# The last block of a hybrid encoder kernel: its output projection split into a GLA half and a convolution half

## The chip, the core and the metric

The kernel runs on one core of one Trainium2 chip. The metric is the device time of one execution in microseconds (us), lower being better; three executions of the kernel before took 1037.42, 1040.89 and 1041.53 us.

## What is computed

One step of an encoder layer over 2048 prompt frames and 64 sample frames of width 1024. A normed input goes through one input projection; three groups of heads work on parts of it; each is gated, and one output projection joins them. Cut to the parts that matter here:

```python
def mixer_layer(x, ...):
    proj = rmsnorm(x, norm_g) @ w_in
    ...
    y_attn = band_attention(q, k_all, v_all, sinks, q_pos0) * jax.nn.silu(ag)
    o, s_fin = gla_chunked(gq * GLA_DK ** -0.5, gk, gv, log_a, gla_s0)
    y_gla = rmsnorm(o, gla_g).reshape(B, L, GLA_VDIM) * jax.nn.silu(gg)
    u = cv * jax.nn.sigmoid(cgl)
    c = depthwise_conv(u_all, conv_w) + conv_b            # 31 taps over time, 256 channels
    c = jax.nn.silu(layernorm(c, ln_g, ln_b)) @ w_pw + b_pw
    y_conv = c * jax.nn.silu(cg)
    y = jnp.concatenate([y_attn, y_gla, y_conv], axis=-1) @ w_out
    return x + y, ...
```

The output projection is a sum over the rows of `w_out`: 512 rows belong to attention, 256 to GLA (gated linear attention) and 256 to the convolution.

## The kernel before

It makes two passes. The first works through tiles of 128 frames: norm, attention and the attention rows of the output projection, whose result, with `x` added, is stored in the output. The second works through `NB` = 8 blocks of 256 frames: the projections of GLA and convolution, both mixers, and the other 512 rows of `w_out`, whose result is added to what the first pass stored. Each fp32 product is made of three products of rounded halves (hi by hi, hi by lo, lo by hi), so one bank of the output projection, 128 frames by 512 columns, takes 12 matmuls: four row groups `k` of 128 (0 and 1 are GLA, 2 and 3 convolution), three products each. A block has four such banks (two tiles of frames, two halves of the columns).

Each engine has its own program, written out by hand in a loop over `b` from 0 to `NB`, and runs it strictly in that order; semaphores join them. In round `b` an engine interleaves the work of block `b` ("cur") with the end of block `b - 1` ("done", "prev"). In the last round, `b` = 8, nothing is current: what is left is the end of the last block alone, as a chain through four engines. In the order of that chain, with the functions that issue it:

- `o_sums`, `o_rinv`, `o_norm`: sums, inverse root and scaling of the GLA output (VectorE, GpSimd, VectorE); between them VectorE does the last 14 of the 62 convolution steps of the block (`conv(p, 48, 52)`, `conv(p, 52, 62)`), into `acc`.
- `conv_T`: four TensorE transposes of `acc` into bank `S0`; `o_T`: four of the normed GLA output `on` into `T2`.
- `ln_stats`, `ln_rinv`: layer norm statistics (VectorE, GpSimd).
- `y_gla`, `y_hi`, `y_lo`: the gated GLA output and its two halves `ybg` (tiles `ybgh`, `ybgl`; VectorE, ScalarE, VectorE).
- `ln_scale`: the scaled layer norm, written over `on` (its name there is `cn`) once `ybgl` is done; `cn_T`: four transposes of it into `S1`.
- `conv_silu`, `conv_gate`: scale, tanh and product (ScalarE, VectorE); `pointwise`: the product with `w_pw` into `T2`.
- `y_conv`, `y_hi`, `y_lo`: the gated convolution output and its halves `ybc` (`ybch`, `ybcl`).
- `output_b`: the four banks of the output projection, each with all 12 matmuls; `add`: the sum with the rows loaded into `res`; `store_out_b`: the store, issued by SyncE.

The `J` banks are handed round by a list (`ORDER`), three of them, each filled again once VectorE has emptied it. `o_T` before waits in TensorE's program behind `conv_T`, and every output matmul behind both halves:

```python
                if i == 0 and h == 0:
                    pe.wait_ge(yg_lo, groups_before(b + 1))
                    pe.wait_ge(yc_lo, groups_before(b + 1))
```

Of the kernel before, what the change touches and what calls it, by code (L numbers as in the profile page):

```python
# [33 lines left out]
P = 128  # L34
D = 1024
# [9 lines left out]
CW = 31  # L45
# [16 lines left out]
NB = SEQ // 256  # L62
WIDE = 256 + DEC
U0, U1 = HIST, HIST + 256 + HIST
UB = U1 + DEC
# [122 lines left out]
def build(nc, ins, consts, x_T, outs):  # L188
# [13 lines left out]
    with es:  # L202
# [57 lines left out]
        eb = ExitStack()  # L260
        xbraw = sb("xbraw", [P, KT, WIDE], F32, eb)
        eb.close()
        xbl = sb("xbl", [P, KT, WIDE], F32R)
# [111 lines left out]
        k_taken = sem("gla_k_taken")  # L375
        xb_loaded, params_ready = sem("x_pair_loaded"), sem("params_ready")
        states_stored, u_stored, u_copied = sem("states_stored"), sem("u_stored"), sem("u_copied")
        gv_taken, lr_psum, lr_T = sem("v_taken"), sem("lowrank_psum"), sem("lowrank_T")
# [142 lines left out]
        def load_res_b(b, i):  # L521
# [3 lines left out]
            nc.sync.dma_start(res[n % 2][rows, :], src).then_inc(B.res_loaded[n % 2], 16)  # L525

        def store_out_b(b, i):
            n = tile_no(b, i)
            for h in range(2):
                cols = slice(h * 512, (h + 1) * 512)  # L530
                nc.sync.wait_ge(B.out_added, 2 * n + h + 1)
                rows, dst = out_rows(b, i, cols)
                nc.sync.dma_start(dst, res[n % 2][rows, cols]).then_inc(B.out_stored[n % 2], 16)

# [111 lines left out]
        def go_count(g):  # L646

            gi, _, _, own = g
            return own[-1] + 1 if gi < 2 else tile_no(gi - 1, own[-1]) + 1

        def on_y(g):
# [10 lines left out]
        def bank_of(kind, b, i):  # L662

            return J[BANK[kind, b, i]]

# [9 lines left out]
        def empty_bank(kind, b, i):  # L675

            n = ORDER.index((kind, b, i))
            if n >= 3:
                nc.tensor.wait_ge(*emptied(*ORDER[n - 3]))
            return bank_of(kind, b, i)  # L680
# [12 lines left out]
        def _(sp):  # L693
# [59 lines left out]
            for b in range(NB + 1):  # L753
# [37 lines left out]
        def _(pool):  # L791
# [57 lines left out]
            for b in range(NB + 1):  # L849
                for g in groups(b - 1):  # L850
                    o_rinv(g)
                for g in groups(b - 1):
                    ln_rinv(g)
                if b < NB:
                    for n in range(4):
                        gate(b, n)


        @block.scalar
        def _(act):  # L860
# [223 lines left out]
            def conv_silu(g):  # L1084
                gi, off, w, own = g
                if gi == 0:
                    act.wait_ge(consts_b, N_CONSTS_B)
                bank = T[0] if own == (2,) else S[1]
                act.wait_ge(cnT_psum, gi + 1)
# [20 lines left out]
            for b in range(NB + 1):  # L1110
                cur, done = b < NB, groups(b - 1)
                for g in done:
# [40 lines left out]
                if cur:  # L1153
                    take_kend(b)
                    if b == 0:
                        act.wait_ge(zeros_b, 5)
                    q_blocks(b)
                if b + 1 < NB:
                    split_pair_hi(b + 1, 0)
                    split_pair_hi(b + 1, 1)  # L1160
# [3 lines left out]
        def _(dve):  # L1164
# [238 lines left out]
            def y_gla(g):  # L1403
                gi, off, w, own = g
                b = max(gi - 1, 0)
                dve.wait_ge(oT_psum, gi + 1)
                dve.wait_ge(gate_done, 4 * b + 2)
                nc.vector.scalar_tensor_tensor(on_y(g), T[2][:, :].rearrange("p (j n) -> p j n", n=256)[:, :, 0:w],
                                               glagain[:, 0:1], ggate[:, :, off:off + w], ALU.mult, ALU.mult).then_inc(
                                                   yg_ready, 1)  # L1410
# [19 lines left out]
            def ln_scale(g):  # L1430
# [3 lines left out]
                dve.wait_ge(ln_r, gi + 1)  # L1434
                dve.wait_ge(yg_lo, gi + 1)
                for n, i in enumerate(own):
                    last = nc.vector.tensor_scalar(cn[rows, i, :], bank[rows, 256 * n:256 * n + 256], mv[rows, i, 0:1],
                                                   rs[rows, i:i + 1], ALU.subtract, ALU.mult)
# [96 lines left out]
            def add(b, i, h):  # L1535
                n = SLOT["out", b, 2 * i + h]
                m = tile_no(b, i)
                rows = slice(DEC, P) if i == 2 else slice(0, P)
                if h == 0:
                    dve.wait_ge(B.res_loaded[m % 2], 16 * (m // 2 + 1))  # L1540
                dve.wait_ge(slot_done, n + 1)
                dst = res[m % 2][rows, h * 512:(h + 1) * 512]
                nc.vector.tensor_tensor(dst, bank_of("out", b, 2 * i + h)[rows, :], dst, ALU.add).then_inc(B.out_added, 1)
# [7 lines left out]
            for b in range(NB + 1):  # L1551
                p = b - 1
                cur, prev, done = b < NB, b > 0, groups(b - 1)
                for g in done:
                    o_sums(g)
                if prev:
                    conv(p, 48, 52)
# [4 lines left out]
                if cur and b > 0:  # L1562
                    glu(b, 0)
                if prev:
                    conv(p, 52, 2 * CW)
# [15 lines left out]
                if cur:  # L1581
                    conv(b, 0, 3)
                if b == 0:
# [5 lines left out]
                if cur:  # L1589
                    conv(b, 3, 16)  # L1590
                for g in done:
                    if g[3] != (2,):
                        conv_gate(g)
                if cur:
                    conv(b, 16, 18)
                    logit_parts(b)
# [3 lines left out]
                if cur:  # L1600
                    conv(b, 18, 22)
                    decay_sums(b)
# [6 lines left out]
                if cur:  # L1609
                    conv(b, 22, 30)  # L1610
                if b == 1:
# [3 lines left out]
                if cur:  # L1615
                    k_scaled(b)
                    conv(b, 30, 33)
                    q_scaled(b)
                    conv(b, 33, 36)
                    q_full(b)  # L1620
# [4 lines left out]
                if cur:  # L1625
                    conv(b, 36, 40)
                if b == 0:
# [6 lines left out]
                if b == 0:  # L1634
# [6 lines left out]
                    state(b, 2)  # L1641
                    conv(b, 40, 48)
                elif cur:
                    if b + 1 < NB:
                        split_pair_lo(b + 1, 0)
                    add(p, 1, 0)
                    if b + 1 < NB:
                        split_pair_lo(b + 1, 1)
                    conv(b, 40, 42)
# [14 lines left out]
        def _(pe):  # L1664
# [163 lines left out]
            def output_b(b, i, h):  # L1828
# [12 lines left out]
                last.then_inc(slot_done, 1)  # L1841

            def o_T(g):
                gi, off, w, own = g
                pe.wait_ge(go_n, gi + 1)
                need(pe, yg_ready, gi)
                rows = min(w, P)
                for n, i in enumerate(own):
                    for j in range(CJ):
                        last = nc.tensor.transpose(T[2][:, j * 256 + n * P:j * 256 + n * P + rows],  # L1850
                                                   on[0:rows, i, j * P:(j + 1) * P], ident[0:rows, 0:rows])
                last.then_inc(oT_psum, 1)

            def conv_T(g):
# [4 lines left out]
                if own == (2,):  # L1859
                    pe.wait_ge(yg_ready, gi + 1)  # L1860
                rows = min(w, P)
                for n, i in enumerate(own):
# [6 lines left out]
            def cn_T(g):  # L1869
                gi, off, w, own = g  # L1870
                bank = T[0] if own == (2,) else S[1]
                pe.wait_ge(cn_ready, gi + 1)
                rows = min(w, P)
                for n, i in enumerate(own):
                    for j in range(CJ):
                        last = nc.tensor.transpose(bank[:, j * 256 + n * P:j * 256 + n * P + rows],
                                                   cn[0:rows, i, j * P:(j + 1) * P], ident[0:rows, 0:rows])
                last.then_inc(cnT_psum, 1)

            def pointwise(g):  # L1880
                gi, off, w, own = g
                pe.wait_ge(cs_ready, gi + 1)
                pe.wait_ge(yg_ready, groups_before(max(gi - 1, 0) + 1))
                need(pe, yc_ready, gi)
                pe.wait_ge(cn_ready, groups_before(max(gi - 1, 0) + 1))
                for j in range(CJ):
                    for k in range(CJ):
# [77 lines left out]
            for b in range(NB + 1):  # L1965
                p = b - 1
                cur, prev, done = b < NB, b > 0, groups(b - 1)
                if cur and b > 0:
# [137 lines left out]
```

## Time and profile before

| what | value |
|---|---|
| median of three executions | 1040.89 us (1037.42 to 1041.53) |
| the profiled execution, its own time | 1040.45 us |
| its span in the profile | 1038.7 us |
| TensorE busy | 965.1 us, 93% of the span |
| VectorE busy | 771.2 us, 74% |
| mean granted TensorE clock | 0.964 of full |

The span runs from the first to the last instruction on record; the time of the execution is 1.75 us more than it. [...] In rows of matmuls, busy times of neighbours overlap, so that the start of one to the start of the next is what each costs.

### The profile page before, as it was taken

The page shows a single profiled execution, that of the slowest core. Times are in us where ns is not written, and L with a number is a line of the kernel's source. Part 1 is how long each engine was busy: PE and PEld are TensorE (multiplying, and loading weights), DVE is VectorE, ACT ScalarE, POOL GpSimd, SP SyncE. Part 2 cuts the span into 40 slices and gives each one's busy share as a digit, 9 for nine tenths or more (in the row PEclk, how much of TensorE's full clock was granted, in tenths as well). Part 3 has the DMA queues.
Part 4 walks back from the last instruction along what each step waited for, and adds up shares of the span by engine and source line. Part 5 has one row for each costly group of instructions (what it writes and reads, how often), then busy time and mean ns, then how long its engine had stood idle before and what let it go on. Part 6 is the DMA issues. An engine that isn't in the chain of part 4 may idle for free.

```text
span 1038.7 us, 15969 instructions
## 1 busy us (share of the span) xinstructions
PE 965.1 (93%) x5835; PEld 842.1 (81%) x5835; DVE 771.2 (74%) x1864; ACT 466.2 (45%) x1131; POOL 186.2 (18%) x216
## 2 busy tenths in 40 slices
PE   6769999999999999997989887999999999999956
PEld 5657888888888888886987776998989898989945
DVE  6477777777777777778679677788888888878772
ACT  7266666556656655556654034041423324150400
POOL 0312211222211222210012131020202111121210
PEclk9879999999999999999999798999999999999977
DMA  9412222222222222134342102303030212111021
GB/s 311 172 56 102 102 102 102 94 100 102 102 102 102 102 103 81 62 107 115 95 127 66 47 22 90 93 1 122 1 105 19 71 52 69 54 58 65 1 84 40
DMA packets 57437, 88.37 MB, mean 85 GB/s; under 512 B 9648, under 2 KB 33968, under 8 KB 57360
## 3 DMA queue, kind: packets, MB, share of 16 engines
q1 hardware_dynamic: 57360, 87.36, 25.6%
q8 instruction: 46, 0.75, 0.3%
q14 instruction: 31, 0.25, 0.1%
HBM read 60.80 MB, written 26.60 MB: 84 GB/s over the span
## 4 chain that ended last, share of the span: by engine, by line
PE 79%; DVE 13%; ACT 2%; issue 2%; DMA 2%; POOL 1%; SPq 1%; DVEq 0%; ACTq 0%; POOLq 0%
PE J L619 20%; PE J L1680 18%; PE J L1839 9%; PE J L634 8%; DVE acc L1374 4%; PE J L1824 3%; PE T L1780 3%; PE S L1792 3%; PE S L1748 3%; PE T L1717 2%; PE T L1888 2%; PE S L1960 1%; DMA wraw<-in_w_in 1%; DVE wlo L460 1%; PE T L1726 1%
## 5 line engine op out<-in xcount | busy, mean ns | idle before, releaser
L1374 DVE SCALAR_TENSOR_TENSOR acc<-ub,cwh,acc 128x256 f32<-128x256 f32 (+1 forms) x480 | 222.9, 529 | 0.3
L619 PE MATMUL J<-whi,xhi 128*128 128x512 f32 (+1 forms) x408 | 150.7, 369 | 9.9 <-DVE wlo L460 9.9
L1680 PE MATMUL J<-xbh,whi 128*128 128x256 f32 (+1 forms) x512 | 151.8, 297 | 2.9 <-issue 2.9
L1680 PE MATMUL J<-xbl,whi 128*128 128x256 f32 (+1 forms) x512 | 148.0, 289 | 0.0
L1680 PE MATMUL J<-xbh,wlo 128*128 128x256 f32 (+1 forms) x512 | 147.8, 289 | 0.0
L619 PE MATMUL J<-whi,xlo 128*128 128x512 f32 (+1 forms) x408 | 146.9, 360 | 0.0
L619 PE MATMUL J<-wlo,xhi 128*128 128x512 f32 (+1 forms) x408 | 146.9, 360 | 0.0
L1680 PEld LDWEIGHTS J<-xbh,whi 128*128 128x128 f32 x512 | 98.8, 193 | 6.0 <-issue 5.5
L1680 PEld LDWEIGHTS J<-xbl,whi 128*128 128x128 f32 x512 | 99.0, 193 | 0.2
L1680 PEld LDWEIGHTS J<-xbh,wlo 128*128 128x128 f32 x512 | 98.7, 193 | 0.0
L619 PEld LDWEIGHTS J<-whi,xhi 128*128 128x128 f32 x408 | 78.0, 191 | 20.9 <-DVE xlo L594 9.9
L619 PEld LDWEIGHTS J<-whi,xlo 128*128 128x128 f32 x408 | 77.6, 190 | 12.8
L619 PEld LDWEIGHTS J<-wlo,xhi 128*128 128x128 f32 x408 | 78.1, 192 | 10.3
L925 ACT ACTIVATE sc<-sc,nmx 128x256 f32<-128x256 f32 x136 | 67.6, 500 | 34.5 <-DVE nmx L1202 34.5
L1196 DVE CUSTOM_DVE_ANT_0 sc<-S,bias,sinks 128x256 f32<-128x256 f32 (+1 forms) x136 | 59.2, 471 | 16.6 <-PE S L1748 16.5
L1292 DVE TENSOR_TENSOR ptlo<-T,pthi 128x512 fp32r<-128x512 f32 x68 | 43.9, 687 | 23.5 <-ACT pthi L931 23.5
L584 POOL TENSOR_TENSOR xraw<-xraw,rb 128x1024 f32<-128x1024 f32 x17 | 40.6, 2386 | 103.7 <-ACT rb L578 103.7
L634 PE MATMUL J<-whi,yhi 128*128 128x512 f32 x136 | 56.5, 415 | 0.0
L634 PE MATMUL J<-wlo,yhi 128*128 128x512 f32 x136 | 53.7, 394 | 0.0
L634 PE MATMUL J<-whi,ylo 128*128 128x512 f32 x136 | 53.6, 394 | 0.0
L1780 PE MATMUL T<-ident,sc 128*128 128x128 f32 x272 | 41.9, 289 | 9.6 <-DVE sc L1285 9.6
L1780 PEld LDWEIGHTS T<-ident,sc 128*128 128x128 f32 x272 | 32.8, 145 | 20.0 <-DVE sc L1285 13.5
(235 smaller groups left out, 2226.3 us busy)
## 6 DMA issues: line engine op xcount, KB each, us to landing
out<-res SPq DMA_DIRECT2D x64, 256.0 KB, 2.0
x_normed_scratch<-xraw SPq DMA_DIRECT2D x17, 512.0 KB, 2.9
xraw<-xT SPq DMA_DIRECT2D x16, 512.0 KB, 3.5
xtok<-in_x_prompt SPq DMA_DIRECT2D x16, 512.0 KB, 5.1
res<-in_x_prompt SPq DMA_DIRECT2D x16, 512.0 KB, 5.8
xbraw<-x_normed_scratch SPq DMA_DIRECT2D x16, 512.0 KB, 5.1
res<-out SPq DMA_DIRECT2D x16, 512.0 KB, 4.2
wraw<-in_w_in SPq DMA_DIRECT2D x52, 128.0 KB, 2.5
```

The lines of the kernel that those rows point to most:

```text
L584: nc.gpsimd.tensor_tensor(xraw[t.par][:, :, :], xraw[t.par][:, :, :], rb[:, :].unsqueeze(1).to_broadcast([P, KT, P]), ALU.mult).then_inc(x ...
L619: last = nc.tensor.matmul(bank[:, 0:width], x[x_slot(ps, t)][:, k, :], w, start=(k == 0 and n == 0), stop=(k == KT - 1 and n == 2))
L634: last = nc.tensor.matmul(bank[:, :], y[:, k, :], w, start=(k == 0 and n == 0), stop=(k == 3 and n == 2))
L925: last = nc.scalar.activation(sc[:, h, :], sc[:, h, :], ACT.Exp, bias=nmx[:, h:h + 1], accum_out=esum[:, h:h + 1])
L1196: nc.vector.tensor_tensor_reduce(out=sc[:, h, cols], in0=S[n % 2][:, e * 256:(e + 1) * 256][:, cols], in1=bias[:, h, b0:b0 + 256][:, cols] ...
L1292: nc.vector.tensor_tensor(ptlo[:, k % 2, :], T[k % 3][:, :], f(pthi[:, k % 2, :]), ALU.subtract).then_inc(pt_lo, 1)
L1374: nc.vector.scalar_tensor_tensor(acc[:, j, 0:frames], src, w, acc[:, j, 0:frames], ALU.mult, ALU.add).then_inc(conv_step, 1)
L1680: last = nc.tensor.matmul(bank[:, 0:w], wt, x[:, k, 0:w], start=(k == 0 and m == 0), stop=(k == KT - 1 and m == 2))
L1748: last = nc.tensor.matmul(S[n % 2][:, e * 256:(e + 1) * 256], qT[:, h, :], kT[:, h // GROUP, o, :], start=(o == 0), stop=(o == 1))
L1780: last = nc.tensor.transpose(bank[:, j * P:(j + 1) * P], sc[:, GROUP * g + j, n * P:(n + 1) * P], ident[:, :])
L1792: last = nc.tensor.matmul(S[g][:, :], vcat[n][:, g, :], pt[:, n, :], start=(n == 0 and m == 0), stop=(n == 1 and m == 1))
L1839: last = nc.tensor.matmul(bank[:, :], y[:, k % 2, at:at + P], wt, start=(k == 0 and m == 0), stop=(k == 3 and m == 2))
```

## The change

TensorE's last round is a function of its own, `output_end`. It transposes the GLA output first, then the convolution; it begins the output projection with the GLA rows of three banks as soon as `ybgl` is ready; then come `cn_T`, the GLA rows of the fourth bank, `pointwise`, and at the end the convolution rows of all four banks. So that four sums can be open at once, the fourth takes `S0` in place of a `J` bank. `o_T` goes into `T1`, `cn_T` into `T0`, and the scaled layer norm is written into `acc`. The residual rows of the last block are loaded into the idle input buffer `xbraw` (as `res_end`) in round 7, in place of `res` in round 8. The rest of the chain of the last block moves, on ScalarE, VectorE and GpSimd, from round 8 of the loop to the end of round 7.

```diff
@@ SyncE, round 7
-                for i in tiles(p)[0:2]:
+                for i in tiles(p)[0:2] if b < NB else []:
                     load_res_b(p, i)
...
+                if b == NB - 1:
+                    sp.wait_ge(slot_done, SLOT["gq", b, 0] + 1)
+                    for i in range(2):
+                        load_res_end(i)
@@ VectorE, end of round 7
+                elif b == NB - 1:
+                    g = groups(b)[0]
+                    add(p, 1, 0)
+                    conv(b, 40, 42)
+                    state(b, 0)
+                    conv(b, 42, 45)
+                    add(p, 1, 1)
+                    conv(b, 45, 48)
+                    state(b, 1)
+                    o_sums(g)
+                    conv(b, 48, 52)
+                    o_norm(g)
+                    conv(b, 52, 2 * CW)
+                    ln_stats(g)
+                    y_gla(g)
+                    y_lo(g, on_y(g), ybg, 4.0, yg_hi, yg_lo)
+                    ln_scale(g)
+                    conv_gate(g)
+                    y_conv(g)
+                    y_lo(g, cl[:, :, 0:256], ybc, 0.25, yc_hi, yc_lo)
@@ TensorE
+            def output_end(b):
+
+                o_T(groups(b)[0])
+                conv_T(groups(b)[0])
+                pe.wait_ge(yg_lo, groups_before(b + 1))
+                for s in (0, 1, 2):
+                    output_half(empty_bank("out", b, s), s // 2, s % 2, (0, 1))
+                cn_T(groups(b)[0])
+                output_half(empty_bank("out", b, 3), 1, 1, (0, 1))
+                pointwise(groups(b)[0])
+                pe.wait_ge(yc_lo, groups_before(b + 1))
+                for s in range(4):
+                    output_half(bank_of("out", b, s), s // 2, s % 2, (2, 3)).then_inc(slot_done, 1)
+
+            def output_half(bank, i, h, ks):
+
+                for k in ks:
+                    hi, lo = weights(W_OUT + k * D + h * 512, 512)
+                    yh, yl = (ybg, ybc)[k // 2]
+                    for m, (y, wt) in enumerate(((yh, hi), (yh, lo), (yl, hi))):
+                        last = nc.tensor.matmul(bank[:, :], y[:, k % 2, i * P:(i + 1) * P], wt,
+                                                start=(k == 0 and m == 0), stop=(k == 3 and m == 2),
+                                                skip_group_check=True)
+                return last
```

TensorE's program from the last GLA product of block 7 on, before (`S<-ident,acc` is `conv_T`, `T<-ident,on` is `o_T`, `S<-ident,on` is `cn_T`, `T<-cth,params` is `pointwise`, the `J` rows are `output_b`; the rows behind the last shown repeat its pattern for three more banks):

```order
L1960 MATMUL S<-gvt,asb 128x64 x4
L1865 MATMUL S<-ident,acc 128x128 x4
L1850 MATMUL T<-ident,on 128x128 x4
L1876 MATMUL S<-ident,on 128x128 x4
L1888 MATMUL T<-cth,params 128x256 x4
L1839 MATMUL J<-whi,ybgh 128x512
L1839 MATMUL J<-wlo,ybgh 128x512
L1839 MATMUL J<-whi,ybgl 128x512
...
L1839 MATMUL J<-whi,ybch 128x512
L1839 MATMUL J<-wlo,ybch 128x512
L1839 MATMUL J<-whi,ybcl 128x512
```

The same place now (each "..." stands for more matmuls of the three rows ahead of it, 18 in all in the first case, 6 in the second; `T<-ident,acc` is now `cn_T`, since the scaled norm lies in `acc`):

```order
L2046 MATMUL S<-gvt,asb 128x64 x4
L1930 MATMUL T<-ident,on 128x128 x4
L1947 MATMUL S<-ident,acc 128x128 x4
L1915 MATMUL J<-whi,ybgh 128x512
L1915 MATMUL J<-wlo,ybgh 128x512
L1915 MATMUL J<-whi,ybgl 128x512
...
L1960 MATMUL T<-ident,acc 128x128 x4
L1915 MATMUL S<-whi,ybgh 128x512
L1915 MATMUL S<-wlo,ybgh 128x512
L1915 MATMUL S<-whi,ybgl 128x512
...
L1974 MATMUL T<-cth,params 128x256 x4
L1915 MATMUL J<-whi,ybch 128x512
```

Of the 48 output matmuls 24 now stand ahead of `pointwise`, and 18 of these ahead of `cn_T`.

VectorE's program from the last ten convolution steps on, before:

```order
L1374 SCALAR_TENSOR_TENSOR acc<-ub,cwh,acc 128x256 [waits conv_step] x10
L1423 BN_STATS bst<-S 128x6 [waits cT_psum]
L1427 BN_AGGR mv<-bst 128x2 [waits ln_step]
L1408 SCALAR_TENSOR_TENSOR on<-T,params,ggate 128x512 [waits gate_ready_b,gla_oT_psum]
L1415 SCALAR_TENSOR_TENSOR ybgl<-on,ybgh 128x2x256 [waits gla_y_hi]
L1437 TENSOR_SCALAR on<-S,mv,rs 128x256 [waits gla_y_lo,ln_rinv]
```

And now:

```order
L1404 SCALAR_TENSOR_TENSOR acc<-ub,cwh,acc 128x256 [waits conv_step] x10
L1453 BN_STATS bst<-S 128x6 [waits cT_psum]
L1457 BN_AGGR mv<-bst 128x2 [waits ln_step]
L1438 SCALAR_TENSOR_TENSOR on<-T,params,ggate 128x512 [waits gate_ready_b,gla_oT_psum]
L1445 SCALAR_TENSOR_TENSOR ybgl<-on,ybgh 128x2x256 [waits gla_y_hi]
L1467 TENSOR_SCALAR acc<-S,mv,rs 128x256 [waits gla_y_lo,ln_rinv]
```

Nothing has moved here: VectorE's program has the same instructions in the same order from its first to its last, and only the tiles that `ln_scale` and the last four `add` write are others. The same holds for ScalarE and GpSimd.

## Rows read from the trace of the kernel before

**Rows 1.** The page: the granted clock in 40 equal slices, in tenths of full.

```profile
PEclk9879999999999999999999798999999999999977
```

**Rows 2.** Stretches: length, busy PE, PEld, DVE, ACT, POOL; PEclk, DMA share, GB/s.

```profile
939.40:995.00 55.60, 55.60 (x395) 51.20 (x395) 44.43 (x109) 14.93 (x37) 9.50 (x12) 1.00 0.11 39
995.00:1038.70 43.70, 22.67 (x87) 17.40 (x85) 19.74 (x44) 3.50 (x6) 3.03 (x4) 0.73 0.16 55
```

**Rows 3.** The chain that ended last: start us, length us, what.

```profile
963.85 0.43 PE S L1876 x4
...
970.78 1.73 PE T L1888 x8
...
981.00 2.75 PE J L1839 x12
...
1003.55 3.97 DVE acc L1374 x10
...
1011.10 0.70 DVE ybgl L1415
...
1011.89 1.01 DVE on L1437 x2
...
1012.95 1.13 PE S L1876 x4
...
1016.56 3.80 PE T L1888 x8
...
1020.38 0.89 DVE cl L1453 x2
...
1022.79 12.70 PE J L1839 x48
...
1035.51 0.69 DVE res L1543
```

**Rows 4.** The timeline of the last 35 us: start us, us, engine, line, what.

```profile
1008.47 1.06 PE L1850 MATMUL T<-ident,on 128*128 128x128 f32 x4
...
1009.68 0.72 DVE L1408 SCALAR_TENSOR_TENSOR on<-T,params,ggate 128x512 f32<-128x512 f32 x1
...
1023.35 0.63 PE L1839 MATMUL J<-wlo,ybgh 128*128 128x512 f32 x1
...
1025.49 0.59 PE L1839 MATMUL J<-whi,ybch 128*128 128x512 f32 x1
...
1026.38 0.39 PE L1839 MATMUL J<-whi,ybch 128*128 128x512 f32 x1
...
1035.09 0.39 PE L1839 MATMUL J<-whi,ybcl 128*128 128x512 f32 x1
```

**Rows 5.** Short stretches around changes of the granted clock, columns as in group 2.

```profile
27.00:28.00 1.00, 0.00 (x0) 0.00 (x0) 0.17 (x1) 0.47 (x3) 0.74 (x2) 1.00 0.51 149
...
37.00:38.00 1.00, 0.39 (x4) 0.19 (x2) 0.56 (x1) 1.00 (x5) 0.00 (x0) 1.00 0.00 0
...
39.00:40.00 1.00, 0.00 (x0) 0.00 (x0) 1.00 (x1) 0.00 (x0) 1.00 (x1) 0.73 0.97 385
40.00:41.00 1.00, 0.14 (x1) 0.17 (x2) 0.91 (x2) 0.00 (x0) 0.56 (x1) 0.50 1.07 414
...
46.00:47.00 1.00, 1.00 (x5) 0.78 (x5) 0.00 (x0) 0.27 (x2) 0.57 (x2) 0.86 0.92 324
...
70.16:73.57 3.41, 3.41 (x14) 3.02 (x13) 2.67 (x6) 2.51 (x6) 0.56 (x1) 0.50 0.02 5
...
1002.00:1002.50 0.50, 0.00 (x0) 0.00 (x0) 0.12 (x1) 0.00 (x0) 0.50 (x1) 0.52 0.08 17
...
1025.50:1026.00 0.50, 0.50 (x3) 0.40 (x2) 0.00 (x0) 0.00 (x0) 0.00 (x0) 0.59 0.00 0
```

**Rows 6.** The page: DMA issues of the second pass, KB each, us to landing.

```profile
out<-res SPq DMA_DIRECT2D x64, 256.0 KB, 2.0
...
res<-out SPq DMA_DIRECT2D x16, 512.0 KB, 4.2
```

More of the change, by code:

```diff
@@ L261, in build @@
         xbraw = sb("xbraw", [P, KT, WIDE], F32, eb)
+        res_end = [xbraw[:, :, :].rearrange("p k n -> p (k n)")[:, i * D:(i + 1) * D] for i in range(2)]
         eb.close()
@@ L649, in go_count, with cn_of @@
             return own[-1] + 1 if gi < 2 else tile_no(gi - 1, own[-1]) + 1
+        def cn_of(g, i):
+            return acc[:, i, 0:256] if g[0] == END else cn[:, i, :]
         def on_y(g):
@@ L662, in bank_of @@
         def bank_of(kind, b, i):
-            return J[BANK[kind, b, i]]
+            return S[0] if (kind, b, i) == ("out", NB - 1, 3) else J[BANK[kind, b, i]]
         def emptied(kind, b, j):
@@ L677, in empty_bank @@
             n = ORDER.index((kind, b, i))
-            if n >= 3:
+            if n >= 3 and (kind, b, i) != ("out", NB - 1, 3):
                 nc.tensor.wait_ge(*emptied(*ORDER[n - 3]))
@@ L849, in _ @@
             for b in range(NB + 1):
-                for g in groups(b - 1):
+                for g in groups(b - 1) if b < NB else []:
                     o_rinv(g)
-                for g in groups(b - 1):
+                for g in groups(b - 1) if b < NB else []:
                     ln_rinv(g)
@@ L856, in _ @@
                         gate(b, n)
+                if b == NB - 1:
+                    o_rinv(groups(b)[0])
+                    ln_rinv(groups(b)[0])
         @block.scalar
@@ L1087, in conv_silu @@
                     act.wait_ge(consts_b, N_CONSTS_B)
-                bank = T[0] if own == (2,) else S[1]
+                bank = T[0] if own == (2,) or gi == END else S[1]
                 act.wait_ge(cnT_psum, gi + 1)
@@ L1110, in _ @@
             for b in range(NB + 1):
-                cur, done = b < NB, groups(b - 1)
+                cur, done = b < NB, groups(b - 1) if b < NB else []
                 for g in done:
@@ L1434, in ln_scale @@
                 dve.wait_ge(ln_r, gi + 1)
-                dve.wait_ge(yg_lo, gi + 1)
+                need(dve, yg_lo, gi if gi == END else gi + 1)
                 for n, i in enumerate(own):
-                    last = nc.vector.tensor_scalar(cn[rows, i, :], bank[rows, 256 * n:256 * n + 256], mv[rows, i, 0:1],
+                    last = nc.vector.tensor_scalar(cn_of(g, i)[rows, :], bank[rows, 256 * n:256 * n + 256], mv[rows, i, 0:1],
                                                    rs[rows, i:i + 1], ALU.subtract, ALU.mult)
@@ L1552, in _ @@
                 p = b - 1
-                cur, prev, done = b < NB, b > 0, groups(b - 1)
+                cur, prev, done = b < NB, b > 0, groups(b - 1) if b < NB else []
+                at = CONV_END if b == NB - 1 else CONV
+                taps = lambda n: conv(b, at[n], at[n + 1])
                 for g in done:
                     o_sums(g)
-                if prev:
+                if prev and cur:
                     conv(p, 48, 52)
@@ L1563, in _ @@
                     glu(b, 0)
-                if prev:
+                if prev and cur:
                     conv(p, 52, 2 * CW)
@@ L1849, in o_T @@
                     for j in range(CJ):
-                        last = nc.tensor.transpose(T[2][:, j * 256 + n * P:j * 256 + n * P + rows],
+                        last = nc.tensor.transpose(bank[:, j * 256 + n * P:j * 256 + n * P + rows],
                                                    on[0:rows, i, j * P:(j + 1) * P], ident[0:rows, 0:rows])
@@ L1870, in cn_T @@
                 gi, off, w, own = g
-                bank = T[0] if own == (2,) else S[1]
+                bank = T[0] if own == (2,) or gi == END else S[1]
                 pe.wait_ge(cn_ready, gi + 1)
+                if gi == END:
+                    pe.wait_ge(ke_taken, NB)
                 rows = min(w, P)
@@ L1966, in _ @@
                 p = b - 1
-                cur, prev, done = b < NB, b > 0, groups(b - 1)
+                cur, prev, done = b < NB, b > 0, groups(b - 1) if b < NB else []
+                if b == NB:
+                    output_end(p)
+                    break
                 if cur and b > 0:
```

58 lines of the change are left out of this document (40 added, 18 removed).

## The prediction, made before the changed kernel was run

> **What bounds the kernel now.** I read from the whole down to the end. The granted clock in slices is at 0.9 over nearly all of the span, with a dip in the middle, and at 0.7 in the last two slices [rows 1]. The stretches say the same by block: in the last full round TensorE is busy for all of its 55.60 us at full clock, while in the last 43.70 us it is busy for 22.67, at a mean clock of 0.73 [rows 2]. So the second pass is bound by TensorE until about 997, and then comes an end in which nothing overlaps. The change touches only that end, so at most its 43.7 us are at stake, and what matters in it is the chain that ended last.
>
> The chain [rows 3] is to be read as one path through four engines. VectorE's last ten convolution steps end at 1007.52. `ybgl`, the last piece of the GLA output, is done at 1011.80; the scaled norm at 1012.90; `cn_T` runs from 1012.95 for 1.13 us, `pointwise` from 1016.56 for 3.80, `y_conv` starts at 1020.38, and the 48 output matmuls take from 1022.79 to 1035.49. The last addition takes 0.69 us more, and its store lands 2.0 us after its issue [rows 6], which makes the span of 1038.7. Two things stand out. The GLA half of the operand lies ready from 1011.80 and is used only from 1022.79. And TensorE runs at half clock for most of the end: the clock fell at 1002.0 and rose at about 1025.9 [rows 5], so `cn_T` takes 1.13 us where it took 0.43 in the rounds before, `pointwise` 3.80 where it took 1.73 [rows 3], and one output matmul 0.43 us (1023.35 to 1025.49 in five steps) in place of 0.229 (1026.38 to 1035.09 in 38 steps) [rows 4].
>
> **What the change does not do.** The words of the change speak of the convolution interleaved with the GLA chain. The order of VectorE's program shows that it already was: not one instruction moves. So VectorE still reaches the end of its convolution steps at 1007.5 and of `ybgl` at 1011.8. `o_T` is brought ahead of `conv_T`; its operand is ready at 1003.55, when the ten steps begin [rows 3], so it will run there, under 3.97 us of convolution steps. What waited for it was `y_gla`, but that stood behind the layer norm statistics in VectorE's own order: `o_T` ended at 1009.53 and `y_gla` began at 1009.68 [rows 4]. I take 0 for this; if all of the 0.15 between the two were a wait for `o_T`, that would be the gain. Without its cover `o_T` would cost its 1.06 us. The scaled norm goes into `acc`, which takes away its need to wait for the reader of `on`; but in VectorE's order it still stands behind `ybgl`, so it gains nothing.
>
> **The residual loads.** Two loads of 512 KB are put into round 7 of SyncE, behind a wait for the last projection, which ended at 981.00 [rows 3]. Queued behind that wait are the stores of block 6, whose first addition needs a result that is finished only at 983.75, one step of 2.75 us later. A load lands after 4.2 us [rows 6], against more than 40 us until the first use at the end. Cost 0; were the stores of block 6 late by both loads, 8.4 us, they would still be out long before the last four stores, and nothing else waits for them. The loads that they replace were issued after 1002 and were early too. The cover is that slack of 40 us.
>
> **The moved matmuls.** From here I follow the chain anew, from `ybgl` at 1011.80; the first GLA matmul starts at 1011.9, as the others start 0.05 to 0.1 behind their releasers.
>
> 1. Three banks times two row groups times three products: 18 matmuls stand ahead of `cn_T`. At half clock they take 18 x 0.427 = 7.7 us, at full clock 18 x 0.229 = 4.1. The clock rises in between: in the trace it rose at 1025.9, 3.1 us after the dense matmuls began at 1022.79 [rows 3, 5], and early in the kernel at 46.3, 5.4 us after work began again at 40.9 [rows 5]. I take the middle, 4.2 us: 9.8 matmuls at half clock, the other 8.2 in 1.9 us, together 6.1. End 1018.0; the bounds are 5.6 (a rise after 3.1) and 6.6 (after 5.4).
> 2. `cn_T` at full clock: 0.43 us by the round before [rows 3], and with the way to ScalarE 0.6. End 1018.6. It had ended at 1014.1, so this part of the chain is 4.5 us late.
> 3. `conv_silu` and `conv_gate` fill 1014.08 to 1016.56, 2.5 us, on ScalarE and VectorE, unchanged. The fourth bank's six GLA matmuls (6 x 0.229 = 1.4 us) lie under them; without that cover they would cost the 1.4. `pointwise` starts at 1021.1.
> 4. `pointwise` at full clock 1.73 [rows 3] in place of 3.80: end 1022.8.
> 5. `y_conv` and the two halves of its result, 1020.36 to 1022.79, 2.4 us: the 24 convolution matmuls start at 1025.3.
> 6. These 24, all at full clock: 23 steps of 0.229, and from the start of the last (1035.09) to the addition (1035.51) 0.42 [rows 3, 4]: 5.7 us. Each bank takes 1.37 us, more than the 0.69 of an addition, so the additions do not become the bound. The last addition starts at 1031.0, against 1035.51: 4.5 us earlier.
> 7. But TensorE stands idle for the 2.4 us of step 5. In the trace the clock stayed at full over the idle microsecond from 27 to 28, and fell at 39.46, 2.1 us after work stopped at 37.39 [rows 5]. So it probably falls again, in this wait or within about 1.5 us behind it. The shortest spell at half clock with TensorE busy throughout is the one from 70.16 to 73.57, 3.41 us [rows 5]. In it eight output matmuls lose 0.198 each, 1.6 us. Bounds: 0, and two such prices less what the rest of the stretch can hold, 2.5.
>
> Sum of the likeliest case: -4.5 + 1.6 = -2.9 us against the profiled execution, which took 1040.45: 1037.5. The median before is 1040.89. The profiled execution had the earliest rise of the clock seen (3.1 us); with the 4.2 that I gave the changed kernel, its own end would have been 1.1 x 0.46 = 0.5 us longer (each microsecond at half clock loses 1 - 0.229/0.427 = 0.46). So against the median the gain is about 3.4: 1037.5. I say 1037.4.
>
> [...] In these rows no transposition overtakes a matmul that stands ahead of it. [...] Were it otherwise, the 4.5 us of step 2 would come back and the gain would be near 9; I give that no chance of its own. [...]
>
> **The rivals.**
>
> *The clock stays up (26%).* Step 7 costs nothing, because `pointwise` and the GLA matmuls keep TensorE busy enough up to the wait and the matmuls follow soon enough. For it: the idle microsecond at 27. Against it: the fall at 39.46. The gain against the profiled execution is 4.5, with an early rise in step 1 5.0, against the median 5 to 5.5: 1035.6. This is the case that can pass 0.5% (5.2 us), which is about what a measurement of this kernel can tell from no change.
>
> *The queue costs more than the tail gives (7%).* The end on the other side: `cn_T` behind 18 matmuls, with the clock never released before the final stretch. Then step 1 takes 7.7, `cn_T` 1.13, steps 3 and 5 the same, `pointwise` 3.80, and the last 24 matmuls 3.1 us at half clock and 17 at full (7.1 with the end): 1011.9 + 7.7 + 1.15 + 2.5 + 3.8 + 2.4 + 7.1 = 1036.6, 1.1 us later than before, 1041.8. The point from which it decides: the shorter end saves 24 x 0.229 = 5.5 us, so the change loses once steps 1 to 5 together are 5.5 us longer than the 10.99 they took, that is when neither `cn_T` nor `pointwise` finds a full clock. Against it: 7.7 us of dense matmuls are longer than both rises seen. With the last 24 all at half clock as well it would be 3.3 more, 1045, just short of 0.5%.
>
> *Nothing to be seen (10%).* The interleaving is not new, and the gain lies within the scatter of the executions (4.1 us in three runs): 1039 to 1041.
>
> **Chances and range.** The likeliest case, a gain of 2 to 5 us, has 57%; the rivals 26, 7 and 10%. The range reaches from 1034.2 (clock up all through, and a low median) to 1040.2 (the costly bounds of steps 1 and 7, 1.5 + 0.9 us more than the sum). The likeliest case lies within 0.5% by itself, most of the second and third cases too; of the first rival most would pass it only with an early rise or a low draw, and some of the likeliest might by a low draw. That gives faster by over 0.5% 0.22, within 0.5% 0.73, slower 0.05.
>
> **What would show it.** In the profile after: the convolution steps end where they did; `o_T` lies under them; 18 matmuls start within 0.2 us of `ybgl`, and the clock rises among them, 3 to 5.5 us later; `cn_T` starts near 1018, some 5 us after its operand is ready, and takes 0.43; `pointwise` takes 1.73; the last 24 matmuls start near 1025.3 and take 5.7 to 7.3 us. The prediction is wrong if the clock does not rise before `cn_T`, if the additions or stores of the four banks now queue behind one another, or if the loads moved into round 7 delay that round.

## The result

In the comparison made for this change the kernel after took 1033.60 us (median of 6, 1033.03 to 1035.30) against 1040.79 before (median of 6): ratio 0.9945, interval 0.9924 to 0.9967 (the ratio of the means, 1033.99 and 1039.66; that of the medians would be 0.9931). Timed a second time (the run `again` below, 12 executions against 29) it took 1038.50 against 1040.23: ratio 0.9984, interval 0.9970 to 0.9999. The two intervals do not meet, though the kernels are the same, and all six executions of the first timing (up to 1035.30) lie below all twelve of the second (1036.30 to 1039.47). So part of the scatter lies between one timing and the next, and an interval from within one timing is too narrow for it. The profiles show where the difference arises, and what part of the time is the change's.

From the profile of the kernel after, which took 1035.30 us with a span of 1033.5: first the page (the header, TensorE's line and the clock in slices), then two stretches in the columns of [rows 2], the whole end and the time in which the GLA matmuls run.

```profile
span 1033.5 us, 15971 instructions
...
PE 964.5 (93%) x5835; PEld 840.3 (81%) x5835; DVE 772.6 (75%) x1864; ACT 466.3 (45%) x1131; POOL 185.1 (18%) x216
...
PEclk9969999999999999999999888999999999999988
```

```profile
995.00:1033.40 38.40, 20.38 (x75) 15.18 (x74) 17.58 (x40) 3.50 (x6) 3.02 (x4) 0.78 0.10 36
...
1009.00:1018.00 9.00, 8.05 (x28) 6.16 (x28) 1.45 (x4) 1.65 (x3) 0.00 (x0) 0.75 0.00 0
```

The last two slices are at 0.8 of the clock instead of 0.7 [rows 1], and TensorE is busy for 8.05 of the 9 us behind 1009. The same stretch of the kernel before, 2.4 us later, has 4.90 us of work, all at half clock:

```profile
1011.40:1020.40 9.00, 4.90 (x12) 3.24 (x12) 2.09 (x5) 1.65 (x3) 0.00 (x0) 0.50 0.00 0
```

The chain that ended last, with start, length and what, to be held against [rows 3]:

```profile
1001.17 3.97 DVE acc L1404 x10
...
1008.71 0.70 DVE ybgl L1445
...
1009.46 6.22 PE J L1915 x18
1015.68 0.45 PE T L1960 x4
...
1016.15 1.03 ACT cl L1116 x2
...
1018.61 2.01 PE T L1974 x8
...
1020.64 0.89 DVE cl L1483 x2
...
1022.96 6.00 PE J L1915 x18
1028.96 1.39 PE S L1915 x6
...
1030.37 0.69 DVE xbraw L1575
```

To compare it, let each step be counted from the end of `ybgl`, 1011.80 before and 1009.41 after:

| from the end of `ybgl` | before | forecast | after |
|---|---|---|---|
| `cn_T` starts | 1.15 | 6.2 | 6.27 |
| `pointwise` starts | 4.76 | 9.3 | 9.20 |
| last output matmuls start | 10.99 | 13.5 | 13.55 |
| last addition starts | 23.71 | 20.8 (with the fall of the clock) | 20.96 |

So the end is 2.75 us shorter in this profile. The other 2.39 us by which the profiles differ were won before `ybgl`: the sums of the GLA output (`o_sums`) start at 997.47 instead of 999.85, and nothing that the engines run ahead of them has changed its order. That part is looked at below.

The fall of the clock in the last stretch can be read off the steps between output matmuls in the timeline (start, length, engine, line, what):

```profile
1022.96 0.50 PE L1915 MATMUL J<-whi,ybch 128*128 128x512 f32 x1 [2.36 <-DVE ybcl L1445]
...
1023.54 0.51 PE L1915 MATMUL J<-whi,ybcl 128*128 128x512 f32 x1
...
1023.84 0.63 PE L1915 MATMUL J<-whi,ybch 128*128 128x512 f32 x1
...
1024.27 0.63 PE L1915 MATMUL J<-wlo,ybch 128*128 128x512 f32 x1
...
1027.41 0.40 PE L1915 MATMUL J<-whi,ybch 128*128 128x512 f32 x1
```

The first matmul waited 2.36 us for `ybcl`. Steps are 0.43 us from 1023.84 to about 1026.8, where the granted clock is 0.50 (1.00 from 1022.96 to 1023.60 and again from 1027.10 on), then 0.23 again. So the clock fell 0.7 us after the dense work had begun, and it came back 3.4 us later.

The loads moved into round 7 were issued at 978.66, landed after 3.9 us, and no addition waited for them; the stores of block 6 went out at 984.54, as far behind the last projection as before.

### The profile page after: what moved, and what is told of

Same layout as the page of the kernel before. It is cut to its first block, busy times and chain, and to the rows that moved or that the text cites. A ratio compares the mean times of both kernels' runs of the same rounds, so it can differ in the third digit from the quotient of the medians.

```text
span 1033.5 us, 15971 instructions
## 1 busy us (share of the span) xinstructions
PE 964.5 (93%) x5835; PEld 840.3 (81%) x5835; DVE 772.6 (75%) x1864; ACT 466.3 (45%) x1131; POOL 185.1 (18%) x216
## 4 chain that ended last, share of the span: by engine, by line
PE 79%; DVE 13%; ACT 2%; issue 2%; DMA 2%; POOL 1%; SPq 1%; ACTq 0%; DVEq 0%; POOLq 0%
PE J L632 20%; PE J L1732 18%; PE J L647 8%; PE J L1891 8%; DVE acc L1404 4%; PE J L1876 3%; PE T L1832 3%; PE S L1844 3%; PE S L1800 3%; PE T L1769 2%; PE T L1974 1%; PE S L2046 1%; PE J L1915 1%; DVE wlo L465 1%; DMA wraw<-in_w_in 1%
## 5 line engine op out<-in xcount | busy, mean ns | idle before, releaser
L1226 DVE CUSTOM_DVE_ANT_0 sc<-S,bias,sinks 128x256 f32<-128x256 f32 (+1 forms) x136 | 59.1, 471 | 16.6 <-PE S L1800 16.5
L1832 PEld LDWEIGHTS T<-ident,sc 128*128 128x128 f32 x272 | 32.8, 145 | 20.0 <-DVE sc L1315 13.5
```

Source lines behind the costliest of these rows:

```text
L1226: nc.vector.tensor_tensor_reduce(out=sc[:, h, cols], in0=S[n % 2][:, e * 256:(e + 1) * 256][:, cols], in1=bias[:, h, b0:b0 + 256][:, cols] ...
L1832: last = nc.tensor.transpose(bank[:, j * P:(j + 1) * P], sc[:, GROUP * g + j, n * P:(n + 1) * P], ident[:, :])
```

## Experiments

A measure that leaves the scatter ahead of the end out: the time from the start of the GLA sums to the start of the last addition, in the profile of each kernel. Between the two lie all the steps that the change touches.

| kernel | sums start at | sums to last addition | against before | timed ratio (interval) |
|---|---|---|---|---|
| before | 999.85 | 35.66 | | |
| after | 997.47 | 32.90 | -2.8 | 0.9945 (0.9924 to 0.9967) |
| `again` | 1000.42 | 33.28 | -2.4 | 0.9984 (0.9970 to 0.9999) |
| `rest_only` | 1000.70 | 35.18 | -0.5 | 0.9996 (0.9981 to 1.0011) |
| `twice` | 999.25 | 38.28 | +2.6 | 1.0034 (1.0019 to 1.0049) |
| `fill_waits` | 1000.96 | 27.80 | -7.9 | 0.9936 (0.9915 to 0.9957) |
| `fourth_in_wait` | 1000.02 | 31.54 | -4.1 | 0.9965 (0.9950 to 0.9980) |
| `norm_first` | 995.31 | 31.63 | -4.0 | 0.9961 (0.9946 to 0.9976) |
| `gla_early` | 1000.04 | 27.43 | -8.2 | 0.9929 (0.9908 to 0.9950) |

The program ahead of the sums is the same in all rows but the first, yet they start anywhere from 995.3 to 1001.0. That is the scatter in which a gain of 3 us has to be found. In the seven lower rows the timed gain and that of the stretch differ by at most 1.2 us; in the first timing of the change by 2.9. All diffs below are against the changed kernel.

### again: the changed kernel once more

No edit.

> The changed kernel as it is, timed once more. From the sums of the GLA output to the last addition it took 32.9 us in its profile against 35.7 before, so 2.8 us come from the end; the other 2.4 us of the profiled difference lie ahead of round 7, where the program is the same. Theory: those 2.4 us are scatter of the clock in the first 100 us and around the change of passes, and a new timing gives 2.5 to 4.5 us, a ratio of 0.996 to 0.9975. Rival: something ahead of the end is really faster, and the ratio is again 0.9945 or below.

The ratio, 0.9984, is above the range that I gave, 0.996 to 0.9975 (its interval, 0.9970 to 0.9999, reaches into it), and far from the rival's 0.9945. The end took 33.28 us in its profile, 2.4 less than before; the sums started at 1000.42, 2.95 us later than in the first profile of the same program. So about half of the first gain of 5.7 us was not the change's: an earlier start of the end, which the second timing does not have. Aligned instruction by instruction, VectorE in the first profile of the changed kernel is 2.4 us ahead of the kernel before at 40.6, 4.5 at 51.5, 0.8 at 631 and 2.4 from 647 on, then constant up to the sums: the difference arises in the first 100 us and around the change of passes. That it comes from the clock, as my theory had it, is not shown. The mean granted clock of the first 560 us is 0.97 in the profile that is ahead and 0.98 in that of before, and 0.88 in both from 560 to 660. The cause stays open.

### rest_only: everything but the order on TensorE

```diff
-                o_T(groups(b)[0])
                 conv_T(groups(b)[0])
-                pe.wait_ge(yg_lo, groups_before(b + 1))
-                for s in (0, 1, 2):
-                    output_half(empty_bank("out", b, s), s // 2, s % 2, (0, 1))
+                o_T(groups(b)[0])
                 cn_T(groups(b)[0])
-                output_half(empty_bank("out", b, 3), 1, 1, (0, 1))
                 pointwise(groups(b)[0])
+                pe.wait_ge(yg_lo, groups_before(b + 1))
                 pe.wait_ge(yc_lo, groups_before(b + 1))
                 for s in range(4):
-                    output_half(bank_of("out", b, s), s // 2, s % 2, (2, 3)).then_inc(slot_done, 1)
+                    output_half(empty_bank("out", b, s), s // 2, s % 2, (0, 1, 2, 3)).then_inc(slot_done, 1)
```

> The changed kernel with TensorE's last round in the order of before (convolution and GLA transposes, then all 48 output matmuls behind both halves); the early residual loads, the use of acc, T0, T1 and S0 stay. Theory: these cost and gain nothing, 35.7 us from the GLA sums to the last addition (34.2 to 37.2 with the clock), ratio 1.000. Rival: a part of the gain is theirs, 2 us or more, ratio 0.998 or below.

Ratio 0.9996, and 35.18 us against 35.66: as expected. From its chain that ended last:

```profile
1012.55 1.00 DVE acc L1467 x2
1013.55 0.05 issue
1013.59 1.13 PE T L1957 x4
...
1017.21 3.40 PE T L1971 x8
1020.61 2.40 issue
1023.01 10.08 PE J L1912 x36
```

Of the 0.5 us, 0.4 are `pointwise`, during which the clock rose (3.40 us against 3.80). The last stretch gives 0.15 back (12.87 us against 12.72): the clock was up at its start and fell 0.5 us into it. The other 0.2 are the change's own, and the prediction had put them at nothing: the scaled norm starts 11.85 us behind the sums, against 12.04 before. Before, it is written over the tile that `ybgl` reads, so VectorE waits for `ybgl` and starts 0.10 us behind its end. Written into `acc` it waits only for the `ybgl` of the group before (`need(dve, yg_lo, gi if gi == END else gi + 1)`), and in the changed kernel it starts 0.08 us ahead of that end: at 1009.32, with `ybgl` from 1008.71 for 0.69. Apart from these 0.2 us the early loads, the other banks and `acc` are worth nothing that can be seen. They are what allows the order.

### twice: the GLA matmuls early, and once more at the end

```diff
-                    output_half(bank_of("out", b, s), s // 2, s % 2, (2, 3)).then_inc(slot_done, 1)
+                    output_half(bank_of("out", b, s), s // 2, s % 2, (0, 1, 2, 3)).then_inc(slot_done, 1)
```

> The changed kernel, but the 24 GLA matmuls are done early and thrown away, and all 48 are done at the end. Theory: the shorter end is worth 24 x 0.229 = 5.5 us, so this takes 32.9 + 5.5 = 38.4 us from the GLA sums to the last addition, 2.7 us more than before, ratio 1.0026. Rival: it is the clock, kept up by the early matmuls, that gives the gain, and the place of the work matters little: 33 to 35.5 us, ratio 0.998 to 1.000.

38.28 us, 1.0034: the first theory, to 0.1 us. This kernel has the clock of the changed kernel in all places, the late `cn_T` as well, and loses; so the gain is the work taken out of the last stretch, 24 matmuls. What the clock gives back (`cn_T` 0.45 instead of 1.13, `pointwise` 2.01 instead of 3.80, 2.5 us together) only pays for half of the 5.0 us by which `cn_T` starts late.

### fill_waits: the same matmuls, placed into the waits

```diff
                 conv_T(groups(b)[0])
+                cn_T(groups(b)[0])
                 pe.wait_ge(yg_lo, groups_before(b + 1))
-                for s in (0, 1, 2):
+                for s in (0, 1):
                     output_half(empty_bank("out", b, s), s // 2, s % 2, (0, 1))
-                cn_T(groups(b)[0])
-                output_half(empty_bank("out", b, 3), 1, 1, (0, 1))
                 pointwise(groups(b)[0])
+                for s in (2, 3):
+                    output_half(empty_bank("out", b, s), s // 2, s % 2, (0, 1))
                 pe.wait_ge(yc_lo, groups_before(b + 1))
```

> The changed kernel with another order on TensorE: the transposes of the scaled norm first, then 12 GLA matmuls, the product with w_pw, the other 12 GLA matmuls in the wait for the gated convolution output, then the 24 of the convolution. Theory: the transposes no longer stand 5.2 us behind 18 matmuls, and 12 matmuls fill a wait of 2.4 us: cn_T ends at 2.1 us after ybgl, pointwise starts at 7 and ends at 9 to 11, the last 24 start at 11.7 to 13.7 and take 5.7: 29.3 us from the GLA sums to the last addition (up to 31.5 with a half clock at pointwise), ratio about 0.994. Rival: the clock, which now rises later or falls within, eats the gain: 32.5 us or more, ratio as of the changed kernel.

27.80 us, below the 29.3 to 31.5 expected; 1.3 of the 1.5 us are the first twelve matmuls, which took 3.78 us instead of 5.1 at half clock throughout. Its chain that ended last:

```profile
1013.85 1.11 PE T L1961 x4
1014.96 3.78 PE J L1916 x12
1018.74 1.73 PE T L1975 x8
1020.46 1.39 PE J L1916 x6
1021.85 1.37 PE S L1916 x6
1023.22 4.12 PE J L1916 x18
1027.34 1.39 PE S L1916 x6
```

From `cn_T` to the end it is TensorE alone, with no gap: the chain through ScalarE and VectorE is hidden under GLA matmuls twice. `cn_T` still runs at half clock (1.11), the clock rises within the first twelve (12 steps in 3.78 us), and it stays up to the end. Two stretches in the columns of [rows 2] say the same, the wait for `y_conv` and the last 24:

```profile
1020.46:1023.22 2.76, 2.76 (x14) 2.25 (x13) 1.56 (x3) 0.63 (x1) 0.00 (x0) 1.00 0.00 0
1023.20:1029.00 5.80, 5.52 (x25) 4.18 (x23) 2.31 (x4) 0.00 (x0) 0.00 (x0) 1.00 0.24 90
```

### fourth_in_wait: six matmuls moved behind `pointwise`

```diff
                 cn_T(groups(b)[0])
-                output_half(empty_bank("out", b, 3), 1, 1, (0, 1))
                 pointwise(groups(b)[0])
+                output_half(empty_bank("out", b, 3), 1, 1, (0, 1))
```

> The changed kernel with one thing moved: the fourth bank's six GLA matmuls stand behind the product with w_pw, in the wait of 2.4 us for the gated convolution output, in place of ahead of it. Theory: that product waits for ScalarE and VectorE anyway, so it starts as before, and the six matmuls (1.4 us) fill the wait; TensorE's clock, which fell within the last stretch in both profiles of the changed kernel, stays at full, and the last 24 matmuls take 5.7 us in place of 7.4: 31.3 us from the GLA sums to the last addition, against 32.9 and 33.3. Rival: the product itself meets half a clock, or the clock falls anyway: 33 us or more.

31.54 us and 0.9965: the theory. `pointwise` started 9.4 us behind `ybgl` and took 2.01, as in the changed kernel; TensorE worked for 1.37 of the wait, and the last 24 matmuls then ran at full clock:

```profile
1023.40:1025.70 2.30, 1.37 (x6) 0.76 (x5) 1.56 (x3) 0.63 (x1) 0.00 (x0) 1.00 0.00 0
1025.70:1031.50 5.80, 5.77 (x24) 4.43 (x24) 2.08 (x3) 0.00 (x0) 0.00 (x0) 1.00 0.24 90
```

Moving 1.4 us of work from one hidden place to another took 1.4 to 1.7 us off the end, by the clock alone. (5.83 us for these 24, against 7.41 in both profiles of the changed kernel.) This is one profile against two; by the timed intervals alone, 0.9950 to 0.9980 against 0.9970 to 0.9999, the two kernels can't be told apart.

### norm_first: the norm's transposes ahead of all GLA matmuls

```diff
                 conv_T(groups(b)[0])
+                cn_T(groups(b)[0])
                 pe.wait_ge(yg_lo, groups_before(b + 1))
-                for s in (0, 1, 2):
+                for s in range(4):
                     output_half(empty_bank("out", b, s), s // 2, s % 2, (0, 1))
-                cn_T(groups(b)[0])
-                output_half(empty_bank("out", b, 3), 1, 1, (0, 1))
                 pointwise(groups(b)[0])
```

> The changed kernel with the transposes of the scaled norm ahead of all 24 GLA matmuls, and these all ahead of the product with w_pw. Theory: the chain is no longer late at the transposes, but at the product, which now stands behind 24 matmuls: they take 6.4 us from 14.0 (counted from the GLA sums; 12 took 3.8 in the last profile), so the product starts at 20.5 and ends at 22.2, the last matmuls start at 24.7 and take 5.7 to 7.4: 30.4 to 32.1 us, between the changed kernel (32.9) and the one that fills both waits (27.8). Rival: taking the queue from in front of the transposes gives nearly all of the 5.1 us by which that one is better: 28.5 or less.

31.63 us, within the range, though the 24 matmuls took 7.72 us instead of 6.4: the last stretch, 5.82 us, lay at the short end of the 5.7 to 7.4 that the range left open. The queue has only moved: 24 matmuls stand in front of `pointwise`, which starts at 21.73 us behind the sums, against 21.14 in the changed kernel, whereas it could have started near 16.5.

```profile
1008.20 1.12 PE T L1959 x4
1009.32 6.32 PE J L1914 x18
1015.64 1.40 PE S L1914 x6
1017.04 1.74 PE T L1973 x8
...
1021.12 4.41 PE J L1914 x18
```

It is 1.3 us better than the changed kernel all the same, because the clock rose once and stayed. It stayed although the wait ahead of them was as long as in the changed kernel, with nothing in it:

```profile
1018.80:1021.10 2.30, 0.00 (x0) 0.00 (x0) 1.57 (x3) 0.63 (x1) 0.00 (x0) 1.00 0.00 0
1021.10:1026.90 5.80, 5.78 (x24) 4.43 (x24) 2.08 (x3) 0.00 (x0) 0.00 (x0) 1.00 0.24 90
```

So that wait by itself, 2.30 us with nothing in it, did not bring the clock down. What makes `fill_waits` another 3.8 us better is the split around `pointwise`.

### gla_early: the GLA chain within the convolution steps

```diff
@@ VectorE
                     o_norm(g)
-                    conv(b, 52, 2 * CW)
-                    ln_stats(g)
+                    conv(b, 52, 55)
                     y_gla(g)
+                    conv(b, 55, 57)
                     y_lo(g, on_y(g), ybg, 4.0, yg_hi, yg_lo)
+                    conv(b, 57, 2 * CW)
+                    ln_stats(g)
                     ln_scale(g)
@@ TensorE
                 o_T(groups(b)[0])
-                conv_T(groups(b)[0])
                 pe.wait_ge(yg_lo, groups_before(b + 1))
-                for s in (0, 1, 2):
-                    output_half(empty_bank("out", b, s), s // 2, s % 2, (0, 1))
+                output_half(empty_bank("out", b, 0), 0, 0, (0, 1))
+                conv_T(groups(b)[0])
+                output_half(empty_bank("out", b, 1), 0, 1, (0, 1))
                 cn_T(groups(b)[0])
-                output_half(empty_bank("out", b, 3), 1, 1, (0, 1))
+                output_half(empty_bank("out", b, 2), 1, 0, (0, 1))
                 pointwise(groups(b)[0])
+                output_half(empty_bank("out", b, 3), 1, 1, (0, 1))
```

> The changed kernel with the GLA output chain moved up on VectorE, between its last ten convolution steps, ahead of the layer norm statistics, and on TensorE one bank's six GLA matmuls ahead of the convolution transposes, one behind them, one behind the transposes of the norm, one behind the product with w_pw. Theory: the convolution steps end 1.4 us later by the two moved operations, but the scaled norm no longer waits for them, so it comes within 0.5 us of where it was, about 11.9 us after the GLA sums; the matmuls lie in waits, and the clock is up earlier: 26.5 us, at most 28.5 with a half clock at the transposes or the product, ratio 0.991 to 0.993. Rival: the bank ahead of the convolution transposes holds them up at half clock (2.6 us), and nothing is won over the order that fills the waits: 28 us or more.

27.43 us: 0.9 worse than my theory, 0.4 better than `fill_waits`, and by the timed ratios (0.9929 and 0.9936) not to be told from it. The timeline shows what I had left out:

```profile
1007.01 2.07 DVE L1404 SCALAR_TENSOR_TENSOR acc<-ub,cwh,acc 128x256 f32<-128x256 f32 x5
...
1009.87 1.06 PE L1950 MATMUL S<-ident,acc 128*128 128x128 f32 x4
...
1010.97 0.76 DVE L1453 BATCH_NORM_STATS2 bst<-S 128x6 f32<-128x256 f32 x2 [1.89 <-PE S L1950]
...
1013.10 0.99 DVE L1467 TENSOR_SCALAR acc<-S,mv,rs 128x256 f32<-128x256 f32 x2 [1.09 <-POOL rs L858]
```

`conv_T` stands behind six matmuls at half clock (steps of 0.43 us, granted clock 0.50) and starts 0.8 us after the last step, and the norm now waits 1.09 us for GpSimd's inverse root, which `y_gla` and `y_lo` used to cover. The scaled norm starts 13.06 us behind the sums instead of 11.85.

## Why the prediction came out as it did

**The end: right, term by term.** The forecast gave 2.9 us against the profiled execution. The profile has 2.75 (2.4 in that of `again`), and the steps lie where the table above shows. The 18 matmuls took 6.22 us (forecast 6.1), with the rise 4.0 us behind their start (4.2; 4.7 and 6.59 us for the 18 in the profile of `again`); `cn_T` 0.45 (0.43); the last stretch 7.41 to the addition (5.7 + 1.6). Too small by 0.3 was only `pointwise`, 2.01 instead of 1.73. Behind a row of matmuls it took 1.73 and 1.74 (`fill_waits`, `norm_first`), and 2.01 in the five profiles in which TensorE had stood idle in front of it, for 1.11 or 2.49 us, with the clock up (after, `again`, `twice`, `fourth_in_wait`, `gla_early`).

**What costs nothing: right, but for one small term.** `o_T` ran under the ten convolution steps, VectorE's program did not move, the loads hid; `rest_only` shows it in one number. Only the scaled norm in `acc`, of which the prediction says that it gains nothing, starts 0.2 us earlier; in the changed kernel this is hidden, since `cn_T` waits for the 18 matmuls.

**The rivals.** The clock did fall, in both profiles, within the last stretch, and `fourth_in_wait` shows what the fall costs: 7.41 - 5.83 = 1.6 us, as forecast. The reason given, that TensorE stands idle for the 2.4 us ahead of that stretch, is only a part of it. There are two waits in front of that stretch, one ahead of `pointwise` and one behind it. For how many us TensorE stood idle in each, in all profiles in which the clock was up when the last stretch began:

| kernel | idle ahead of `pointwise` | idle behind it | clock in the last stretch |
|---|---|---|---|
| after, `again`, `twice` | 1.1 | 2.4 | fell after 0.6 to 1.1 us |
| `rest_only` | 2.5 | 2.4 | fell after 0.5 us |
| `fourth_in_wait` | 2.5 | 1.0 | stayed |
| `gla_early` | 1.1 | 1.0 | stayed |
| `norm_first` | 0 | 2.3 | stayed |
| `fill_waits` | 0 | 0 | stayed |

It fell where the second wait was whole and TensorE had stood idle in the first too; it stayed where the second was shortened or the first closed. Each order but one has a single profile, so this is a pattern and not a rule; what decides it is open. By its total alone (1035.6) the rival in which the clock stays up would look best in the first timing, 1033.6: the profile shows that it did not happen, and the number came from the scatter ahead of the end. The case on the other side, the queue costing more than the tail gives, did not occur, since the clock rose within the 18; `twice` shows how near it is: with the same clock and no shorter tail the change would lose 2.6 us. That `cn_T` waits out all 18 though its operand is ready, as step 2 has it, can be read from `o_T` before: ready at 1003.55, it ran at 1008.47, behind `conv_T`, which began at 1007.56 [rows 3, 4]. The ends of all nine profiles agree, TensorE's matmuls standing in them in the order of the program: `cn_T`, whose operand was ready at 1010.3 in the kernel after, ran at 1015.68, behind all 18.

**The time: 1037.4 forecast; 1033.6 in the first timing, 1038.5 in the second.** The first median lies 0.6 below the range (1034.2 to 1040.2), the second within it. What was mis-sized is the bound "clock up all through, and a low median": it gave the scatter ahead of the end too little. The upper bound does not follow from its own terms either: step 1 gives 6.6 - 6.1 = 0.5 us on the costly side, not 1.5, and with 0.9 from step 7 the sum is 1038.8. The ratio of the first timing puts the gain at 5.7 us (3.4 to 7.9), that of the second at 1.7 (0.1 to 3.1); the profiles of the same program give 2.4 to 2.8 for the end. The forecast of 3.4 against the median lies between the two timings, but how near the total came is luck: the end was forecast, and the scatter ahead of it is as large as the gain. By the second timing alone, with a gain of 0.1 to 3.1 us, the rival "nothing to be seen" would be nearly as good. The forecast included 0.5 us for an earlier rise of the clock in the profiled execution before than on average. That term is below anything measured here and stays open.

**Where the rest of the possible gain went.** The change has the right idea and about a third of its worth. The last stretch went from 12.72 to 7.41 us, 5.3 less: 5.5 for the 24 matmuls, 1.4 because it no longer begins with seven steps at half clock, and 1.6 lost again to the fall. Against these 5.3 stand 2.6 net for the queue in front of `cn_T` (5.1 late, 2.5 back by the clock). `fill_waits`, with the same 24 matmuls in other places, gains 7.9 us in its profile against 2.8 and 2.4, and 0.9936 against 0.9984 when both were timed together.

## What to carry to other kernels

When independent work is pulled ahead to fill an idle engine, put it into the waits of the critical chain, not in front of its next short instruction: in the changed kernel four transposes, 0.45 us together, were ready at 1010.3 and waited 5.4 us behind 18 matmuls, in the order of the program. Look at the granted clock of the dense stretch that follows: with TensorE idle for 1.1 and 2.4 us in the two waits ahead of it, it fell and cost 1.6 us; with the second shortened or the first closed it stayed up. And where the change is at the end of a long program, measure a stretch of the profile between two fixed instructions: ratios of the whole time moved by 0.4% between two timings of the same two kernels, further than their intervals allow, and the stretch by 0.4 us.

## What the runs showed of the hardware

- The granted clock showed two levels only, 0.50 and 1.00, in the ends of all nine profiles; one output matmul took 0.43 us at the first and 0.23 at the second. In the changed kernel TensorE stood idle for 1.11 and 2.36 us on either side of a `pointwise` of 2.01, and the clock fell 0.7 us into the dense stretch behind; with 1.37 us of work within the second wait, or with the first one closed and the second as it was (`norm_first`), it stayed up.
- The changed kernel reached the sums of the GLA output, some 96% of the way through, at 997.47 and 1000.42 us; over all eight kernels that are the same up to there, the times go from 995.31 to 1000.96.
- An instruction of VectorE started 0.08 us ahead of the end of the one before it where it waited for nothing of that one, and 0.10 us behind that end where it waited for its semaphore (the scaled norm behind `ybgl`).
- The product with `w_pw`, fp32, took 1.73 us behind other matmuls (`fill_waits`, 1.74 in `norm_first`) and 2.01 behind a TensorE idle for 1.11 us (the kernel after) or 2.49 (`fourth_in_wait`), at a granted clock of 1.00 in all four.
